# Three small edits of engine order in a one-core two-block network: unread products, a second root, turned values

## The reference

```python
def rms_norm_2(x, w):
    xf = x.astype(jnp.float32)
    y = xf * lax.rsqrt(jnp.mean(xf * xf, axis=-1, keepdims=True) + EPS)
    return (y * w.astype(jnp.float32)).astype(x.dtype)
...
    for l in range(DEPTH_2):
        h = h + 0.5 * swiglu(rms_norm_2(h, ffn1_norm[l]), ffn1_w_in[l], ffn1_w_out[l])
        u = rms_norm_2(h, mix_norm[l])
        (z_s, xbc, dt_s, qkv, z_d, b_d, a_d, gate_s, gate_d) = jnp.split(u @ w_in[l], split_points, axis=-1)
        y_s = mamba2_branch(z_s, xbc, dt_s, ...)
        y_d = deltanet_branch(qkv, z_d, b_d, a_d, ...)
...
# mamba2_branch: gate with z, then a norm over each of 4 groups of channels
    yg = (y.reshape(b, S, SSM_INNER) * jax.nn.silu(z.astype(f32))).reshape(b, S, SSM_GROUPS, -1)
    yg = yg * lax.rsqrt(jnp.mean(yg * yg, axis=-1, keepdims=True) + EPS)
...
# deltanet_branch: queries and keys of 8 heads are normed, then a chunked recurrence
    q = l2_norm(q.reshape(b, S, DN_HEADS, DN_HEAD_K)) * (DN_HEAD_K ** -0.5)
    k = l2_norm(k.reshape(b, S, DN_HEADS, DN_HEAD_K))
```

## Time and profile before

| | us |
|---|---|
| median of 3 runs | 2162.71 |
| lowest and highest of them | 2161.74, 2163.32 |
| the profiled execution's own time | 2163.85 |
| its span, from the first to the last instruction | 2162.0 |

### The profile page before, as it was taken

The page is one execution under the profiler, slowest core; times in us unless marked ns, Lnnn a source line. Parts: engine busy times, 40 slices in busy tenths (PEclk is TensorE's granted clock), DMA queues, the critical chain, the costliest instruction groups (busy, mean ns, idle before and its releaser), DMA issues.

```text
span 2162.0 us, 39555 instructions
## 1 busy us (share of the span) xinstructions
PE 2115.2 (98%) x15650; PEld 1853.3 (86%) x15650; DVE 1335.5 (62%) x1846; ACT 1150.1 (53%) x1713; POOL 70.1 (3%) x88
## 2 busy tenths in 40 slices
PE   7999999999999999989999999999999998999998
PEld 5888888888889998889998888888998898998887
DVE  3447565565557986676555556555997675756555
ACT  3454754455446576655445445445557663535444
POOL 1000000000000020200000000000002010000000
PEclk9999999999999999999999999999999999999999
DMA  9763255545554544422555555554554431445553
GB/s 377 292 251 127 98 182 187 183 174 195 193 179 154 178 164 153 150 80 80 185 184 202 177 191 177 192 189 161 176 177 156 157 117 40 157 177 193 187 183 125
DMA packets 53459, 373.10 MB, mean 173 GB/s; under 512 B 6320, under 2 KB 6448, under 8 KB 9424
## 3 DMA queue, kind: packets, MB, share of 16 engines
q1 hardware_dynamic: 47808, 342.00, 43.8%
q0 software_dynamic: 5520, 29.23, 3.9%
HBM read 370.10 MB, written 1.11 MB: 172 GB/s over the span
## 4 chain that ended last, share of the span: by engine, by line
PE 90%; DVE 4%; ACT 2%; issue 1%; DMA 1%; POOL 1%; SPq 0%; DVEq 0%; ACTq 0%; POOLq 0%
PE banks L567 14%; PE banks L565 14%; PE banks L566 14%; PE banks L511 10%; PE banks L512 10%; PE banks L513 10%; PE banks L621 4%; PE banks L675 1%; DVE LO L2148 1%; PE banks L650 1%; PE banks L732 1%; PE banks L655 1%; PE banks L651 1%; DMA ARENA<-in_ada_stream 1%; PE banks L1146 1%
## 5 line engine op out<-in xcount | busy, mean ns | idle before, releaser
L1533 ACT ACTIVATE HI<-ring 128x1024 fp32r<-128x1024 f32 x606 | 625.8, 1055 | 700.9 <-PE banks L567 395.1
L2142 DVE TENSOR_TENSOR LO<-ring,HI 128x1024 fp32r<-128x1024 f32 x334 | 409.0, 1227 | 367.4 <-ACT HI L1533 367.1
L2148 DVE TENSOR_TENSOR LO<-ring,HI 128x2048 fp32r<-128x2048 f32 x134 | 307.3, 2293 | 191.6 <-ACT HI L1533 191.6
L511 PE MATMUL banks<-UH,HI 128*128 128x256 f32 x1456 | 423.6, 291 | 0.8 <-DVE LO L2148 0.6
L512 PE MATMUL banks<-UL,HI 128*128 128x256 f32 x1456 | 411.6, 283 | 0.0
L513 PE MATMUL banks<-UH,LO 128*128 128x256 f32 x1456 | 411.5, 283 | 0.0
L565 PE MATMUL banks<-HI,UH 128*128 128x512 f32 x896 | 349.0, 390 | 0.0
L567 PE MATMUL banks<-HI,UL 128*128 128x512 f32 x896 | 348.6, 389 | 0.0
L566 PE MATMUL banks<-LO,UH 128*128 128x512 f32 x896 | 348.6, 389 | 0.0
L511 PEld LDWEIGHTS banks<-UH,HI 128*128 128x128 f32 x1456 | 278.6, 191 | 17.2 <-issue 15.4
L512 PEld LDWEIGHTS banks<-UL,HI 128*128 128x128 f32 x1456 | 278.8, 192 | 1.9 <-issue 1.7
(11 more groups left out here) (356 smaller groups left out, 2996.9 us busy)
## 6 DMA issues: line engine op xcount, KB each, us to landing
ring<-in_w_stream SPq DMA_DIRECT2D x315, 1024.0 KB, 4.8
ARENA<-in_ada_stream POOLq DMA_DIRECT2D x16, 1024.0 KB, 7.7
ARENA<-in_ada_stream SPq DMA_DIRECT2D x8, 1024.0 KB, 13.6
GRMS<-cum_rows POOLq DMA_DIRECT2D x16, 256.0 KB, 3.5
ARENA<-in_na_bias POOLq DMA_DIRECT2D x2, 1024.0 KB, 11.9
RMS<-cum_rows POOLq DMA_DIRECT2D x8, 256.0 KB, 3.6
RSTD<-cum_rows POOLq DMA_DIRECT2D x8, 256.0 KB, 3.7
ARENA<-in_ropes POOLq DMA_DIRECT2D x1, 1088.0 KB, 10.1
```

The costliest lines, as they stand in the source:

```text
L511: nc.tensor.matmul(out, lh, rh, start=start, stop=False, **kw)
L1533: nc.scalar.activation(HI[:, q % PARTS, at], ring[:, q % RING, at], ACT.Copy).then_inc(hi_ready, 1)
L2142: nc.vector.tensor_tensor(LO[:, q % PARTS, at], ring[:, q % RING, at], HI[:, q % PARTS, at].bitcast(F32), ALU.subtract).then_inc(lo_ready, 1)
L2148: nc.vector.tensor_tensor(LO[:, q % PARTS, :], ring[:, q % RING, :], HI[:, q % PARTS, :].bitcast(F32), ALU.subtract).then_inc(lo_ready, 2)
```

## The change

It makes four edits, for both layers. (1) In front of the norm factors there are two unread products instead of five. (2) The sums of the last tile of queries and keys (`head_sums2(3)`) move from behind z panel 4 to between its two halves; ScalarE's second root moves from round 5 to the end of round 3, VectorE's second reciprocal from round 5 to round 4, and every `group_sum` now waits for the second root. (3) `values_turn(1)` moves from in front of the second late panel to between its halves. (4) VectorE makes the low part of the late panel 2 (`late_low(0)`) before `first_inverse(0)`, and `segments(2)` before `first_inverse(1)`.

```diff
             def spread_scale(n):
 
-                unread_squares(5, 5)
+                unread_squares(5, 2)
                 pe.wait_ge(nrstd_ready, n + 1)
...
                 def group_sum(g):
-                    if g:
-                        pe.wait_ge(qkrms_ready, 2 * l + (2 if g == 3 else 1))
+                    pe.wait_ge(qkrms_ready, 2 * l + 2)
                     pe.wait_ge(ysq_added, 4 * l + g + 1)
...
                         for e in range(2):
+                            if (j, e) == (4, 1):
+                                head_sums2(3).then_inc(qkss_done, 1)
                             wide_half(w0 + L_CONV + j, Q_LAYERS + LQ_WIDE + L_CONV + j, rounds, j % 2, e,
...
-                    if 2 <= j <= 4:
-                        for c in (0, 1) if j == 2 else (j - 1,):
-                            mm = head_sums2(c)
-                        if j % 2 == 0:
-                            mm.then_inc(qkss_done, 1)
+                    if j == 2:
+                        head_sums2(0)
+                        head_sums2(1).then_inc(qkss_done, 1)
+                    if j == 3:
+                        head_sums2(2)
...
                 values_turn(0)
+                late_wide(1, 0)
                 values_turn(1)
-                late_panel(1)
+                late_wide(1, 1)
                 head_products(2)
...
-                    if j in (2, 5):
-                        qk_root(j // 4)
+                    if j in (2, 3):
+                        qk_root(j - 2)
...
-                    if j in (2, 5):
+                    if j in (2, 4):
                         qk_reciprocal(j // 4)
...
                 weights(1)
+                late_low(0)
                 first_inverse(0)
+                segments(2)
                 first_inverse(1)
-                late_low(0)
-                segments(2)
                 weights(2)
```

## The result

| | us |
|---|---|
| before, median of 7 runs on the same chip | 2161.96 |
| after, median of 7 runs | 2167.32 |
| lowest and highest after | 2166.30, 2172.70 |
| after/before, with its 95% interval | 1.0031 [1.0022, 1.0040] |
| the profiled execution's own time, its span | 2166.3, 2164.5 |

The change makes the kernel slower by 5.4 us between the medians, and by 4.8 to 8.6 us by the interval of the ratio, where 1.9 was forecast for it. All times after it lie at 2166.3 or above, and their median lies just inside the forecast range's upper end (2167.4).

What follows compares the result with a forecast made beforehand. TensorE, busy for 98% of the span, was taken as the bound. The terms -1.7 + 3.9 - 2.0 gave +0.2 us, +1.9 with one fall of the clock, so 2164.6 us, range 2161.8 to 2167.4.

Steps and rivals of the forecast that it cites:

- unread products: Before the norm factors: two instead of five products start the spread 0.57 us earlier at three places, -1.7 us.
- the stand, panel 4's start to panel 5's, clock apart: Middle of z panel 4: TensorE waits for ScalarE's round 3 squares, so panel 5 starts 2.92 us later per layer.
- the wait behind panel 6 that is gone: Spread behind z panel 6: its 0.96 us wait per layer vanishes, as the second root and reciprocal are long done.
- clock: Behind the stands in z panel 4: one fall of the granted clock in the two layers, +1.7 us.
- turned values: Late panels: half a panel covers VectorE's taking of pieces from the bank, -0.98 us per layer, -2.0 for two.
- the sign of the second edit: Moved sums around z panel 4: a net loss of +1.96 us per layer, +3.9 for two.
- the spread of the norm factors: Norm factors: the spread starts 0.54 us behind the start of the unread products, where it was 1.11.
- the sum by the row: Panel 4's gate: its 1.28 us table load is hidden without a drain; the skill page's drain would add +0.7 us.
- far ahead of panel 6's end: Second reciprocal in round 4: done at about 890.6, while panel 6 ends at about 896.
- the one on what is late next: Behind panel 4: gate, factors' product and reciprocal are in time; between 0 and +1.0 us, taken as 0.
- a rival for round 4: Behind panel 4: gate product takes 1.79 instead of 0.69 us in both layers, +1.0 on the forecast, 2165.6; chance 0.04.
- the rival with a fall in both layers: Behind panel 4's stands: the clock falls in both layers, +3.6 us in all, 2166.3; chance 0.22.

Runs made afterwards that it cites:

- The early squares, with the sums in either place: ScalarE's third-group squares moved to the end of round 5: in the changed kernel 2164.13 us; with the last sums behind panel 4 and the root in round 4, 2155.69 us.
- the squares early: The changed kernel with ScalarE's squares of the third group at the end of round 5 instead of round 6: 2164.13 us.
- the sums alone: The kernel before with only the second edit (last sums between panel 4's halves, earlier second root and reciprocal): 2169.76 us.
- one of 1.33 us: The changed kernel with third-group squares in round 5 and the last sums 12 products later, inside panel 4's second half: 2158.70 us.

## Why the prediction was wrong

The table takes the terms in the order of the prediction, for the whole program, and puts beside them what the profiled execution shows: start to start between rows of before and of after.

| term | predicted | shown |
|---|---|---|
| unread products | -1.7 | 3 x (2.39 - 2.85) = -1.4 |
| the stand, panel 4's start to panel 5's, clock apart | +5.8 | 2 x (12.00 - 7.50 - 1.49) = +6.0 |
| the wait behind panel 6 that is gone | -1.9 | 2 x (13.04 - 14.23) = -2.4 |
| the spread behind panel 7 | 0 | 2 x (7.74 - 6.58) = +2.3 |
| clock | +1.7 | 2 x 1.49 = +3.0 |
| turned values | -2.0 | 2 x (6.62 - 7.63) = -2.0 |
| sum | +1.9 | +5.5 |

The sum of what is shown meets the difference of the medians, +5.4, in part by luck. The two profiled executions differ by 2.5 us of span, and by 4.4 without the early fall of the kernel before. The table holds 1.1 us more than that; 0.8 of it is the delta rule behind the z panels, which was 0.4 us shorter in each layer of the execution after (from high part to high part 56.03 and 55.63 us in layer 0) and is no term here.

**Right.** The stand, its place, its releaser and its length (2.92 forecast, 2.76 waited); the sign of the second edit; the values; the spread of the norm factors (0.55 us against 0.54). The gate of panel 4 with its table load was hidden, as the sum by the row had it: the gate began 0.01 us behind the load, VectorE's gate product there took 0.68 us, and L1180 behind panel 5 had no wait.

```profile
883.22 1.28 ACT L1943 ACT_TABLE_LOAD   x1
884.51 0.60 ACT L1943 ACTIVATE ARENA<-banks 128x512 f32<-128x512 f32 x1
885.51 0.68 DVE L2767 TENSOR_TENSOR ARENA<-ARENA 128x512 f32<-128x512 f32 x1
```

The drain that the Trainium skill, "ScalarE: Activation LUTs", section "What ACT_TABLE_LOAD costs", adds to a switch does not stand on this path.

**Wrong: "far ahead of panel 6's end".** The step that failed is the one on what is late next. It followed the chain of gate product, factors and reciprocal to the spreads behind panels 5 and 6, and stopped; the spread behind panel 7 got no term, and cost 1.09 us of waiting in each layer, +2.3 in the table. The spread behind panel 7 wants the factors' product of round 6. In the kernel before, the table load of round 6 kept GpSimd's addition clear of VectorE's gate product, and the wait behind panel 6 gave VectorE time in hand: its factors' product ended at 898.58 + 1.41 = 899.99, 1.1 us before the spread at 901.11. The change takes both away. The row that shows the price was in the prediction (a gate product of 1.79 us), as a rival for round 4; the collision moved from round 4 to round 6 instead. The early squares, with the sums in either place, show this.

**Mis-sized: the clock.** I took one fall of 1.7 us for two stands. A fall costs 1.49, and the profiled execution had both; the rival with a fall in both layers (2166.3) was nearer. Across executions the number varies: two low half panels in this trace, one with the squares early (layer 1), none in the sums alone. The step from a stand of 2.76 to one of 1.33 us, worth 2.6 us beyond the standing itself, shows that the long stand at this place brings them, 1.7 falls of 1.49 us on average in that kernel.

**Smaller than thought: the unread products.** The spread came as early as forecast, but the five unread products behind it start 0.55 us after it instead of 0.45, so 0.46 us of 0.57 arrive at the next stage.

**Open.** Why twelve more unread products in panel 4 cost some 2 us in the delta rule of layer 1, far behind their place, and lower the clock in most executions, was not settled. Why the one stand is followed by half rate and the other not wasn't tried either. The Trainium skill, "TensorE: Matmul & The Clock Gate", section "Part 1: The HAM clock gate", says that the monitor runs free and doesn't start anew with a kernel. That would leave it to chance, but no run here tests it.

## What to carry to other kernels

Moving a wait earlier is worth nothing if its releaser is a full engine: first ask when the releaser's last work ends, then look for the place in the waiting engine's order that lies just behind it, as the sums behind panel 4 do. When a piece of work is taken out of an engine's round, follow that round to the end of the stage, since everything behind it moves and may meet another engine's work on a shared port; one such meeting cost as much as the wait that was removed. And price an idle stretch amid dense TensorE work with what the clock may add: here 2.76 us of standing cost half as much again where the clock fell behind it, and 1.33 us almost nothing. Products put in to fill a stand are not free beyond their own time either: here they cost some 2 us in a stage that doesn't hold them.

## What was not expected of the hardware

A table load taken away made a later stage slower: without its 1.28 us the squares came 1.4 us earlier in their round, GpSimd's addition went from 1.30 to 2.04 us and VectorE's product from 0.68 to 1.78. And the granted clock came down right behind a stand of 2.76 us with dense panels on both sides of it, where ten of eleven executions with a stand of 1.33 us kept it; and 24 unread products in two panels made a later stage 2.1 us longer at full clock in one kernel, and brought two low stretches there in another.
